# Router logits from un-normalised rows, and an expert's rows modulated as they are read from PSUM

## The chip, the cores and the metric

The kernel runs on one core of one Trainium2 chip. Five engines work side by side: TensorE (PE), VectorE (DVE), ScalarE (ACT), GpSimd (POOL), and SyncE (SP), which issues the weight DMAs. The metric is the device time of one execution in microseconds. Before the change it was 1742.97 us, the median of 3 runs (1740.7 to 1743.19).

## The reference

Two layers act on 256 latent tokens with a prefix of 256 context tokens, D = 1024. Each layer has a token mixer (differential attention beside a spatial gating part) and a channel mixer. In layer 1, the last, only the latent tokens go on, and the channel mixer is a mixture of experts. This is what the change touches:

```python
f_lat = modulate(rmsnorm(x_lat, pre_ffn_g[1]), ms[3], ms[4])     # h * (1 + scale) + shift
logits = t @ router_w                                            # 256 x 8
top_v, top_i = lax.top_k(logits, 2); top_w = softmax(top_v)
for e in range(8):
    y = y + gates[:, e:e+1] * ((silu(t @ w1[e]) * (t @ w3[e])) @ w2[e])     # D_EXPERT = 3584
x_lat = x_lat + ms[5] * rmsnorm(y, post_ffn_g[1])
```

Everything is float32.

## The kernel before

Each float32 product is done as three matmuls on halves of the operands: `hi` is the value rounded to the format fp32r, `lo` is the rest, and the product is hi*hi + lo*hi + hi*lo (`mm3`, L637 to L640). The weights arrive as units of 128x1024 float32 (512 KB, one DMA each). Of each unit ACT writes `w_hi` (L1239, for the experts L1560), DVE writes `w_lo` = unit - `w_hi` (L1657), and PE does 6 matmuls of 512 columns with them. `w_hi` and `w_lo` have SPL = 4 places, so ACT can split a unit only when PE has used the one four before it. For the experts 12 units are in flight from DRAM.

Each engine's order of work is written out by hand, and semaphores join the engines. The order in which the code of an engine calls the helpers below is thus the order in which its instructions run.

The router stage lies between the output projection of layer 1 and the experts. Two blocks of 128 token rows (tb = 0, 1) are normalised: ACT squares the output (L1499), DVE adds two partial sums and makes the mean (L2248, L2249), ACT takes the root (L1502), DVE inverts it and updates `xs` (L1926); then again square (L1257), mean (L1794), root (L1261), inverse and scaling to `xn` (L1799, L1801). PE transposes `xn` (`turn_h`, L710, with `keep_warm` matmuls L700, whose results nobody reads). ACT and DVE modulate the transposed rows, each four of eight 128x256 pieces, into `hT32` (L1314, L2280). PE computes the logits from these (L1076) and transposes the modulated rows back (L1086), and ACT copies them to `hrow` (L1618). `hrow` is what `gather_first` (L1103) and the scatter to DRAM (`xrows`, L619) read. DVE finds the two best experts of each token (L2127 to L2135: `mask_r`), PE counts ranks with small matmuls (L1091 to L1095), and DVE makes from them the 0/1 matrix `perm` of expert 0 (L2141), the rows' places in DRAM (`dest`, L2143 to L2151) and the gates (`token_gates`, L2157 to L2170).

Expert 0's rows come by a matmul with `perm`; those of the experts 1 to 7 are read from `xrows` into `xe` and transposed by PE into two PSUM banks (`gather`, L1130), just before the last four units of the expert ahead (`down(STEPS - 1)`). ACT then copies each bank to `he_hi` (L1541), and DVE subtracts to `he_lo` (L2177). One expert is 84 units: w1 and w3 pieces (`up`), and w2 pieces (`down`) behind them. PE starts an expert with `up(0, 0)`, which waits for unit 0's `w_lo` and for `he_lo`.

Of the kernel before, what the change touches and what calls it, by code (L numbers as in the profile page):

```python
# [17 lines left out]
F32 = mybir.dt.float32  # L18
# [7 lines left out]
P = 128  # L26
# [184 lines left out]
def program(nc, x, ctx, ada_w, ada_b, post_mix_g, post_ffn_g, w_in, w_out,  # L211
# [6 lines left out]
    with ExitStack() as stack:  # L218
# [23 lines left out]
        xs = place("xs", [P, NB, D], F32)  # L242
        cst = place("cst", [P, C_END], F32)
# [55 lines left out]
        rw = place("rw", [P, KD, 32], F32, Z + 36864)  # L299
        hrow = place("hrow", [P, NLAT, D], F32, Z)  # L300
# [4 lines left out]
        triu_r = place("triu_r", [P, P], F32R, H + 28928)  # L305
        ones_r = place("ones_r", [P, P], F32R, H + 29440)
        mask_r = place("mask_r", [P, 2 * NE], F32R, H + 29952)
        perm = place("perm", [P, NLAT, P], F32, H + 30208)
        perm_last = place("perm_last", [P, NLAT, P], F32, H + 31232)
        turned_last = by_expert = perm  # L310
# [130 lines left out]
        def _(sp):  # L441
# [35 lines left out]
            def experts(turn):  # L477
# [4 lines left out]
                def take_x(e):  # L482
                    sp.wait_ge(sg("gathered"), e * 2 + 2 * NE * turn)
                    sp.dma_start(xe[:, :], xv[e][turn]).then_inc(sg("xe in"), 16)
# [50 lines left out]
        def _(pool):  # L535
# [72 lines left out]
            spatial_params(1)  # L608
            spatial_norms(1)
            gate_rows(2)  # L610
            pool.wait_ge(unit_used, NS0)
            link(pool.memset(rw[:, :, :], 0.0))
            pool.dma_start(rw[:, :, 0:NE], router_w[0].rearrange("(k p) e -> p k e", p=P)).then_inc(sg("ws in"), 16)
            pool.wait_ge(sg("rows filled"), 32 * NE + 16)
            pool.wait_ge(sg("hrow"), NLAT)
            pool.wait_ge(sg("dest"), 1)
            for j in range(2):
                for tb in range(NLAT):
                    pool.indirect_dma_start(xrows[:, :], bass.IndirectOffsetOnAxis(ap=dest[:, NLAT * j + tb:NLAT * j + tb + 1], axis=0),  # L619
                                            hrow[:, tb, :], None).then_inc(sg("x sent"), 16)  # L620
# [15 lines left out]
        def _(pe):  # L636
# [64 lines left out]

            def turn_h(key, nb, ks=range(KD)):

                for b in range(nb):
                    if key == "ffn1":
                        keep_warm(12 if b else 6, ps[:, 7, P * b:P * b + P])
                    for k in ks:
                        if k % 4 == 0:
                            pe.wait_ge(sg("xn " + key), b + 1 + (b * k // 4 if key == "ffn1" else 0))
                        m = pe.transpose(ps[:, hT_bank(key, k), P * b:P * b + P], xn[:, b, P * k:P * k + P], ident)  # L710
                        if b == nb - 1:
                            m.then_inc(sg("hT ps " + key), 1)
# [251 lines left out]
            def project_out(l):  # L964
# [35 lines left out]
                pe.wait_ge(sg("z pm%d" % l), 2 * len(out_blocks(l)))  # L1000
# [68 lines left out]

            def route():  # L1070

                pe.wait_ge(sg("ws in"), 16 * 3)
                for k in range(KD):
                    pe.wait_ge(sg("hT32 odd ffn1" if k % 2 else "hT32 ffn1"), k // 2 + 1)
                    q = k % 4
                    m = pe.matmul(ps[32 * q:32 * q + 32, 0, 0:NLAT * P], rw[:, k, :], hT32_late[:, k, 0:NLAT * P], start=(k < 4), stop=(k >= 4),  # L1076
                                  tile_position=(0, 32 * q))
                m.then_inc(sg("logits"), 1)
                for tb in range(NLAT):
                    if tb:  # L1080
                        pe.wait_ge(sg("logits"), 2)
                        for half in range(NLAT):
                            m = pe.transpose(ps[:, half, 0:P], by_expert[:, half, :], ident)
                        m.then_inc(sg("logits"), 1)
                    for k in range(KD):
                        m = pe.transpose(ps[:, 4 + 2 * tb + k // 4, P * (k % 4):P * (k % 4) + P], hT32_late[:, k, P * tb:P * tb + P], ident)  # L1086
                    m.then_inc(sg("hT ps ffn1"), 1)
# [9 lines left out]
            def gather_first():  # L1097
# [3 lines left out]
                for k in range(KD):  # L1101
# [3 lines left out]
                    if k % 4 == 3:  # L1105
                        m.then_inc(sg("gathered"), 1)
# [1257 lines left out]
```

## Time and profile before

| | |
|---|---|
| median of 3 runs | 1742.97 us |
| the profiled execution | 1742.21 us |
| its span | 1740.4 us |
| mean granted clock of TensorE | 0.996 |
| busy: PE, DVE, ACT | 98%, 81%, 63% |
| router stage, end of the output projection to expert 0 at full pace | 757.2 to 783.7 us |
| experts | to about 1724 us |

The span is the part of the execution that the trace covers, here 1.8 us less than the execution's time. A busy PE is not PE at its peak: back to back, 512-column matmuls start every 0.23 us, while each row gives one of them 0.39 us.

### The profile page before, as it was taken

The page shows a single profiled execution, that of the slowest core. Times are in us where ns is not written, and L with a number is a line of the kernel's source. Part 1 is how long each engine was busy: PE and PEld are TensorE (multiplying, and loading weights), DVE is VectorE, ACT ScalarE, POOL GpSimd, SP SyncE. Part 2 cuts the span into 40 slices and gives each one's busy share as a digit, 9 for nine tenths or more (in the row PEclk, how much of TensorE's full clock was granted, in tenths as well). Part 3 has the DMA queues.
Part 4 walks back from the last instruction along what each step waited for, and adds up shares of the span by engine and source line. Part 5 has one row for each costly group of instructions (what it writes and reads, how often), then busy time and mean ns, then how long its engine had stood idle before and what let it go on. Part 6 is the DMA issues. An engine that isn't in the chain of part 4 may idle for free.

```text
span 1740.4 us, 24303 instructions
## 1 busy us (share of the span) xinstructions
PE 1702.7 (98%) x8034; PEld 1380.6 (79%) x8034; DVE 1406.1 (81%) x1655; ACT 1094.9 (63%) x1401; POOL 78.1 (4%) x92
## 2 busy tenths in 40 slices
PE   7999999999999999999999999999999999999997
PEld 4876878888788877778888888888888888888885
DVE  4947677385664589769999999999999999999998
ACT  4435552222222354658888888888888888888886
POOL 0114000000010000310000000000000000000001
PEclk9999999999999999999999999999999999999999
DMA  9858736364574447269999999999999999999995
GB/s 346 281 162 303 265 95 197 105 182 132 157 230 155 126 125 266 75 231 373 383 361 395 385 368 394 376 376 391 366 390 383 362 396 384 369 393 372 381 379 189
DMA packets 229200, 504.73 MB, mean 290 GB/s; under 512 B 16192, under 2 KB 47040, under 8 KB 228848
## 3 DMA queue, kind: packets, MB, share of 16 engines
q1 hardware_dynamic: 225152, 492.78, 79.2%
q0 software_dynamic: 3968, 10.94, 2.1%
q8 instruction: 44, 0.72, 0.2%
q14 instruction: 36, 0.29, 0.0%
HBM read 496.81 MB, written 19.95 MB: 297 GB/s over the span
## 4 chain that ended last, share of the span: by engine, by line
PE 93%; DVE 4%; ACT 1%; issue 1%; DMA 1%; SPq 1%; DVEq 0%; ACTq 0%
PE ps L638 29%; PE ps L640 28%; PE ps L639 28%; PE ps L1161 1%; PE ps L899 1%; PE ps L934 1%; DVE w_lo L1657 1%; DMA raw<-in_ada_w 1%; PE ps L922 0%; PE ps L665 0%; PE ps L658 0%; PE ps L1130 0%; PE ps L685 0%; PE ps L1103 0%; PE ps L882 0%
## 5 line engine op out<-in xcount | busy, mean ns | idle before, releaser
L1657 DVE TENSOR_TENSOR w_lo<-raw,w_hi 128x1024 fp32r<-128x1024 f32 x570 | 685.2, 1224 | 168.4 <-ACT w_hi L1239 141.1
L1560 ACT ACTIVATE w_hi<-raw 128x1024 fp32r<-128x1024 f32 x448 | 473.1, 1061 | 100.3 <-PE ps L640 100.2
L638 PE MATMUL ps<-w_hi,he_hi 128*128 128x512 f32 x896 | 353.7, 395 | 0.8 <-DVE w_lo L1657 0.8
L640 PE MATMUL ps<-w_hi,he_lo 128*128 128x512 f32 x896 | 349.5, 390 | 0.0
L639 PE MATMUL ps<-w_lo,he_hi 128*128 128x512 f32 x896 | 348.8, 389 | 0.0
L1657 DVE TENSOR_TENSOR w_lo<-raw_more,w_hi 128x1024 fp32r<-128x1024 f32 x224 | 273.6, 1225 | 31.1 <-ACT w_hi L1560 12.2
L1560 ACT ACTIVATE w_hi<-raw_more 128x1024 fp32r<-128x1024 f32 x224 | 237.8, 1062 | 50.8 <-PE ps L640 50.8
L1239 ACT ACTIVATE w_hi<-raw 128x1024 fp32r<-128x1024 f32 x122 | 128.4, 1059 | 195.7 <-PE ps L640 182.6
L640 PEld LDWEIGHTS ps<-w_hi,he_lo 128*128 128x128 f32 x896 | 168.2, 188 | 35.9
L638 PEld LDWEIGHTS ps<-w_hi,he_hi 128*128 128x128 f32 x896 | 168.2, 188 | 34.5 <-DVE w_lo L1657 1.2
L639 PEld LDWEIGHTS ps<-w_lo,he_hi 128*128 128x128 f32 x896 | 168.4, 188 | 33.8
L638 PE MATMUL ps<-w_hi,ae_hi 128*128 128x512 f32 x448 | 175.9, 393 | 0.0
L640 PE MATMUL ps<-w_hi,ae_lo 128*128 128x512 f32 x448 | 174.5, 390 | 0.0
L639 PE MATMUL ps<-w_lo,ae_hi 128*128 128x512 f32 x448 | 174.4, 389 | 0.0
L638 PE MATMUL ps<-w_hi,hT_hi 128*128 128x512 f32 x368 | 149.4, 406 | 2.7 <-DVE hT_lo L2057 1.5
L640 PE MATMUL ps<-w_hi,hT_lo 128*128 128x512 f32 x368 | 144.3, 392 | 0.0
L639 PE MATMUL ps<-w_lo,hT_hi 128*128 128x512 f32 x368 | 144.1, 392 | 0.0
L638 PE MATMUL ps<-hT_hi,w_hi 128*128 128x512 f32 x352 | 137.4, 390 | 1.0 <-DVE hT_lo L1825 1.0
L640 PE MATMUL ps<-hT_hi,w_lo 128*128 128x512 f32 x352 | 137.0, 389 | 0.0
L639 PE MATMUL ps<-hT_lo,w_hi 128*128 128x512 f32 x352 | 137.0, 389 | 0.0
L1674 DVE SCALAR_TENSOR_TENSOR acc<-raw,cstat,acc 128x1024 f32<-128x1024 f32 x84 | 105.2, 1280 | 1.7
L640 PEld LDWEIGHTS ps<-w_hi,ae_lo 128*128 128x128 f32 x448 | 84.1, 188 | 17.7
(276 smaller groups left out, 1962.9 us busy)
## 6 DMA issues: line engine op xcount, KB each, us to landing
raw<-in_moe_w SPq DMA_DIRECT2D x448, 512.0 KB, 6.0
raw_more<-in_moe_w SPq DMA_DIRECT2D x224, 512.0 KB, 5.9
raw<-in_ada_w SPq DMA_DIRECT2D x96, 512.0 KB, 4.4
raw<-in_ffn_w SPq DMA_DIRECT2D x66, 512.0 KB, 4.5
raw<-in_w_in SPq DMA_DIRECT2D x40, 512.0 KB, 5.6
raw<-in_w_out SPq DMA_DIRECT2D x16, 512.0 KB, 6.6
yrows<-in_x SPq DMA_DIRECT2D x9, 512.0 KB, 16.3
xe<-xrows SPq DMA_DIRECT2D x7, 512.0 KB, 6.5
```

The costliest lines, as they stand in the source:

```text
L638: pe.matmul(o, lh, rh, start=start, stop=False)
L639: pe.matmul(o, lh, rl, start=False, stop=False)
L640: return pe.matmul(o, ll, rh, start=False, stop=stop)
L899: m = pe.matmul(scores(l, t)[:, m_, :], qT[l][HD * m_:HD * m_ + HD, h, P * b:P * b + P], kT[HD * m_:HD * m_ + HD, h, k0:512], start=True, ...
L934: m = pe.matmul(ps[:, BANK_O, 0:P], wT[:, i % 2, P * kb:P * kb + P], proj[:, kb0 + kb, 2 * DA + P * h:2 * DA + P * h + P], start=(kb == 0) ...
L1161: m = pe.transpose(ps[:, 4 + s % 2, P * j:P * j + P], ae32[:, s % 2, P * j:P * j + P], ident)
L1239: act.activation(w_hi[:, u.s % SPL, :], raw_at(u.k), ACT.Copy).then_inc(hi_done, 1)
L1560: act.activation(w_hi[:, s % SPL, :], expert_raw(i), ACT.Copy).then_inc(hi_done, 1)
L1657: dve.tensor_tensor(w_lo[:, s_ % SPL, :], src, w_hi[:, s_ % SPL, :].bitcast(F32), ALU.subtract)\
L1674: ins = dve.scalar_tensor_tensor(out=total, in0=raw_at(u.k), scalar=cstat[:, k, r:r + 1], in1=total, op0=ALU.mult, op1=ALU.add)
```

## The change

1. **The router.** PE transposes the raw rows `xs` as soon as they are updated (`turn_x`), and not the normalised ones. The first four pieces of a block are copied from PSUM by DVE and the other four by ACT (`keep_xT`). The router's weights are multiplied beforehand by the modulation's scale (`rw_a`), and their product with its shift is summed (`rw_b`, `scale_router`, on DVE in the attention of layer 1). DVE gets the logits as (raw logit) * (1/rms of the row) + (shift's part).
2. **The rows.** What is gathered and scattered is `xn`, normalised but not modulated, so that the transposes back and `hrow` go. Each expert's rows are modulated as ACT reads them from PSUM: eight 128x128 pieces into `he32` in SBUF (Identity with a scale and a bias per partition), then a copy to `he_hi`; DVE subtracts from `he32`.
3. **The order in the router stage.** DVE splits unit 0 between the two blocks' top-2, units 1 to 3 between the pairs of `he_lo`, and makes `dest` and the gates after these. The `keep_warm` matmuls now stand before the ranks and before the gather.
4. **The means.** Wherever DVE made a mean from a sum of squares for ACT's root, ACT's root now takes scale 1/D and a bias (EPS, or the first half's sum prepared earlier by `rest`). This is in all norms but the spatial one and one pair in layer 0.
5. **Router weights** are loaded in layer 1's attention, once the rope tables that they overwrite have been used.

The core of the diff:

```diff
-            for i in range(2):
-                split_expert_unit(i, 0, 0)
-            modulate_h("ffn1", 1, 1, NLAT, range(0, KD, 2))
-            for i in range(2, AHEAD + 1):
-                split_expert_unit(i, 0, 0)
-            for tb in range(NLAT):
-                act.wait_ge(sg("hT ps ffn1"), KD + tb + 1)
-                act.activation(hrow[:, tb, :].rearrange("p (a n) -> p a n", a=2), ps[:, 4 + 2 * tb:6 + 2 * tb, :], ACT.Copy)\
-                    .then_inc(sg("hrow"), 1)
+            norm_before_experts()
+            for i in range(1, AHEAD + 1):
+                split_expert_unit(i, 0, 0)
...
+            def norm_before_experts():
...
+                    if tb:
+                        keep_xT(0)
+                        split_expert_unit(0, 0, 0)
...
+                        act.activation(xn[:, tb, o], xs[:, tb, o], ACT.Square, accum_out=st[:, 4 * half + tb:4 * half + tb + 1])\
+                            .then_inc(sg("ss ffn1"), 1)
+                    if tb:
+                        keep_xT(1)
...
+                act.wait_ge(sg("last rstd"), 1)
+                act.activation(xn[:, 1, :], xs[:, 1, :], ACT.Identity, scale=st[:, 13:14]).then_inc(sg("xn ffn1"), 1)
+
+            def split_first():
+
+                for pair in range(KD // 2):
+                    act.wait_ge(sg("gathered"), pair + 1)
+                    for k in (2 * pair, 2 * pair + 1):
+                        act.activation(he32[:, k, :], ps[:, 4 + pair, P * (k % 2):P * (k % 2) + P], ACT.Identity,
+                                       bias=mod_b[:, 1, 1, k, 0:1], scale=mod_a[:, 1, 1, k, 0:1]).then_inc(sg("he32"), 1)
+                    act.wait_ge(sg("he32"), 2 * pair + 2)
+                    act.activation(he_hi[:, 2 * pair:2 * pair + 2, :], he32[:, 2 * pair:2 * pair + 2, :], ACT.Copy).then_inc(sg("he hi"), 1)
+
+            def split_he(gathered, seen):
...
+                    act.wait_ge(sg("gathered"), gathered + (1 + half))
+                    for k in range(4 * half, 4 * half + 4):
+                        act.activation(he32[:, k, :], ps[:, 2 + half, P * (k % 4):P * (k % 4) + P], ACT.Identity,
+                                       bias=mod_b[:, 1, 1, k, 0:1], scale=mod_a[:, 1, 1, k, 0:1]).then_inc(sg("he32"), 1)
+                    act.wait_ge(sg("he32"), seen + (4 + 4 * half))
+                    act.activation(he_hi[:, 4 * half:4 * half + 4, :], he32[:, 4 * half:4 * half + 4, :], ACT.Copy).then_inc(sg("he hi"), 1)
...
             def pre_root(key, b):
-                act.wait_ge(sg("ms " + key), b + 1)
-                act.activation(st[:, 8 + b:9 + b], st[:, 4 + b:5 + b], ACT.Sqrt).then_inc(sg("rt " + key), 1)
+                act.wait_ge(sg("ss " + key), b + 1)
+                act.activation(st[:, 8 + b:9 + b], st[:, b:b + 1], ACT.Sqrt, scale=1.0 / D, bias=eps).then_inc(sg("rt " + key), 1)
...
+            def logits(tb, ks):
...
+                    m = pe.matmul(ps[:, (6, 3)[tb], 0:P], xT[:, tb, k, :], rw_a[:, k, :].unsqueeze(1).to_broadcast([P, P // NE, NE]),
+                                  start=(k == 0), stop=(k == KD - 1))
...
             def route():
...
+                turn_x(0, 0)
+                turn_x(0, 1)
+                logits(0, range(0, 6))
+                pe.wait_ge(sg("x mix1"), 3)
+                turn_x(1, 0)
+                pe.wait_ge(sg("x mix1"), 4)
+                turn_x(1, 1)
+                logits(0, range(6, KD))
+                logits(1, range(0, 4))
+                logits(1, range(4, KD))
...
+            def scale_router():
...
+                dve.tensor_tensor(rw_a[:, :, :], rw[:, :, :], mod_a[:, 1, 1, :, 0:1].to_broadcast([P, KD, NE]), ALU.mult)
...
+                link(dve.tensor_tensor(parts, rw[:, :, :], mod_b[:, 1, 1, :, 0:1].to_broadcast([P, KD, NE]), ALU.mult))
+                dve.tensor_reduce(rw_b[:, :], parts.rearrange("p k e -> p e k"), AX.X, ALU.add).then_inc(sg("rw scaled"), 1)
...
             def route():
...
+                    dve.wait_ge(sg("logits"), tb + 2)
+                    link(dve.scalar_tensor_tensor(out=lg[:, o], in0=ps[:, (6, 3)[tb], 0:NE], scalar=st[:, 12 + tb:13 + tb], in1=shifted[:, :],
+                                                  op0=ALU.mult, op1=ALU.add))
                     link(dve.max(mx[:, o], lg[:, o]))
                     link(dve.max_index(idx[:, tb, :], mx[:, o], lg[:, o]))
+                    if tb == 0:
...
+                        split_lo(NS0, expert_raw(0), NS0 + 1)
...
+            def split_first():
+
+                for i in range(1, AHEAD + 2):
+                    if i <= AHEAD:
+                        split_lo(NS0 + i, expert_raw(i), NS0 + i + 1)
+                    o = slice(2 * i - 2, 2 * i)
+                    dve.wait_ge(sg("he hi"), i)
+                    dve.tensor_tensor(he_lo[:, o, :], he32[:, o, :], he_hi[:, o, :].bitcast(F32), ALU.subtract).then_inc(sg("he"), 1)
...
+                    split_first()
+                    destinations()
                     token_gates()
```

At the end of an expert ACT ran the following, here for expert 0 (`ps` is PSUM, `ae_hi` the last activations of the expert, `raw` and `raw_more` the places of the units):

```order
L1560 ACTIVATE w_hi<-raw_more 128x1024
L1560 ACTIVATE w_hi<-raw 128x1024 x6
L1595 ACTIVATE ae_hi<-ps 128x512
L1560 ACTIVATE w_hi<-raw 128x1024 x2
L1541 ACTIVATE he_hi<-ps 128x512 x2
```

It now runs:

```order
L1614 ACTIVATE w_hi<-raw_more 128x1024
L1614 ACTIVATE w_hi<-raw 128x1024 x6
L1651 ACTIVATE ae_hi<-ps 128x512
L1614 ACTIVATE w_hi<-raw 128x1024 x2
L1593 ACTIVATE he_117<-ps,mod_b,mod_a 128x128 x4
L1596 ACTIVATE he_hi<-he_117 128x512
L1593 ACTIVATE he_117<-ps,mod_b,mod_a 128x128 x4
L1596 ACTIVATE he_hi<-he_117 128x512
```

The two copies of a bank have become eight modulated pieces and two copies from SBUF, still between the split of the last two units of one expert and of the first of the next.

PE in the router stage, from the end of the output projection to the gather of expert 0, before (`cst` holds the identity, `hT_77` is `hT32`):

```order
L700 MATMUL ps<-cst 128x128 x6
L710 MATMUL ps<-cst,xn 128x128 x8
L700 MATMUL ps<-cst 128x128 x12
L710 MATMUL ps<-cst,xn 128x128 x8
L1076 MATMUL ps<-hT_77,rw 32x256 x8
L1086 MATMUL ps<-cst,hT_77 128x128 x8
L1083 MATMUL ps<-cst,perm 128x128 x2
L1086 MATMUL ps<-cst,hT_77 128x128 x8
L1089 MATMUL ps<-triu_r,ones_r 128x128
```

and now:

```order
L1085 MATMUL ps<-rw_b,cst 128x8
L1067 MATMUL ps<-cst,xs 128x128 x8
L1077 MATMUL ps<-rw_a,xT 128x128 x6
L1067 MATMUL ps<-cst,xs 128x128 x8
L1077 MATMUL ps<-rw_a,xT 128x128 x10
L1098 MATMUL ps<-triu_r,ones_r 128x128
L704 MATMUL ps<-cst 128x128 x6
```

The transposes back and 18 of the matmuls that only keep PE busy (6 and 12) are gone from the front; 6 stand behind the logits, and 3 more behind the ranks.

DVE from the top-2 to the first units, before:

```order
L2141 TENSOR_SCALAR perm<-ps,rs 128x128 x2
L2143 TENSOR_TENSOR rs<-ps,rs 128x16
L2145 TENSOR_TENSOR rs<-rs 128x32
L2147 TENSOR_REDUCE rs<-rs 128x4
L2148 CAST dest<-rs 128x4
L2150 TENSOR_REDUCE rs<-ps 128x1
L2151 CAST flag<-rs 128x1
L1657 TENSOR_TENSOR w_lo<-raw_more,w_hi 128x1024
L2177 TENSOR_TENSOR he_lo<-ps,he_hi 128x512 x2
L1657 TENSOR_TENSOR w_lo<-raw_more,w_hi 128x1024
```

and now (the three `w_lo` are those of the units 1 to 3, each `he_lo` is a pair of 128-column pieces):

```order
L2213 TENSOR_SCALAR perm<-ps,rs 128x128 x2
L1708 TENSOR_TENSOR w_lo<-raw_more,w_hi 128x1024
L2253 TENSOR_TENSOR he_lo<-he_117,he_hi 128x256
L1708 TENSOR_TENSOR w_lo<-raw_more,w_hi 128x1024
L2253 TENSOR_TENSOR he_lo<-he_117,he_hi 128x256
L1708 TENSOR_TENSOR w_lo<-raw_more,w_hi 128x1024
L2253 TENSOR_TENSOR he_lo<-he_117,he_hi 128x256 x2
L2218 TENSOR_TENSOR rs<-ps,rs 128x16
L2219 TENSOR_TENSOR rs<-rs 128x32
```

The making of the rows' places (six rows, L2143 to L2151 before) stood ahead of the split of unit 2 and now begins, in the last two rows, behind unit 3 and the last pair of `he_lo`; the split of unit 0 stands further up, between the two blocks' top-2.

## Rows read from the trace of the kernel before

**Rows 1.** The page: each engine's busy time, share of the span, instructions.
```profile
PE 1702.7 (98%) x8034; PEld 1380.6 (79%) x8034; DVE 1406.1 (81%) x1655; ACT 1094.9 (63%) x1401; POOL 78.1 (4%) x92
```

**Rows 2.** Windows: from:to, length, busy of each engine, granted clock, DMA share, GB/s.
```profile
757.00:765.00 8.00, 6.20 (x53) 5.80 (x53) 5.75 (x13) 4.83 (x10) 1.42 (x2) 1.00 0.06 5
765.00:772.00 7.00, 5.02 (x40) 3.32 (x40) 5.64 (x23) 5.08 (x7) 0.00 (x0) 1.00 0.51 150
772.00:778.00 6.00, 5.93 (x35) 5.87 (x36) 2.69 (x8) 1.05 (x2) 3.52 (x4) 0.72 0.45 113
790.00:880.00 90.00, 90.00 (x410) 74.49 (x409) 84.05 (x77) 72.65 (x76) 0.00 (x0) 1.00 1.03 387
```

**Rows 3.** Chain of waits, 744 to 790: start, length, engine, tile, line.
```profile
756.94 0.24 PE ps L640
...
764.34 1.90 DVE hT L2280 x4
...
770.59 0.27 PE ps L1091
...
772.07 5.45 PE ps L1103 x32
...
782.45 1.24 DVE w_lo L1657
...
783.73 0.50 PE ps L638
```

**Rows 4.** Timeline of DVE in the router stage: start, length, instruction, idle and releaser.
```profile
758.19 0.68 DVE L2251 TENSOR_TENSOR zmix<-ps,gg 128x512 f32<-128x512 f32 x1
...
758.97 1.29 DVE L1926 SCALAR_TENSOR_TENSOR xs<-zmix,st,xs 128x1024 f32<-128x1024 f32 x1
...
771.84 0.17 DVE L2143 TENSOR_TENSOR rs<-ps,rs 128x16 f32<-128x16 f32 x1
...
772.95 1.22 DVE L1657 TENSOR_TENSOR w_lo<-raw_more,w_hi 128x1024 fp32r<-128x1024 f32 x1
...
779.92 0.15 DVE L2157 TENSOR_TENSOR rs<-ps,mask_r 128x2 f32<-128x2 f32 x1
```

**Rows 5.** Timeline of PE, same stage: the matmuls that only keep it busy.
```profile
761.24 2.84 PE L700 MATMUL ps<-cst 128*128 128x128 f32 x24
```

**Rows 6.** Timeline of ACT around the end of expert 0.
```profile
890.16 2.02 ACT L1560 ACTIVATE w_hi<-raw 128x1024 fp32r<-128x1024 f32 x2
892.09 1.07 ACT L1541 ACTIVATE he_hi<-ps 128x512 fp32r<-128x512 f32 x2
893.32 1.06 ACT L1560 ACTIVATE w_hi<-raw_more 128x1024 fp32r<-128x1024 f32 x1 [0.17 <-PE ps L640]
...
897.42 1.06 ACT L1560 ACTIVATE w_hi<-raw_more 128x1024 fp32r<-128x1024 f32 x1 [0.30 <-PE ps L640]
```

**Rows 7.** Timeline of DVE there.
```profile
893.52 1.28 DVE L2177 TENSOR_TENSOR he_lo<-ps,he_hi 128x512 fp32r<-128x512 f32 x2
894.72 5.02 DVE L1657 TENSOR_TENSOR w_lo<-raw_more,w_hi 128x1024 fp32r<-128x1024 f32 x4
```

**Rows 8.** Timeline of ACT in layer 1: modulated and plain 128x256 from PSUM.
```profile
643.92 3.76 ACT L1279 ACTIVATE hT<-ps,mod_b,mod_a 128x256 f32<-128x256 f32 x8 [3.00 <-PE ps L720]
...
738.82 1.21 ACT L1487 ACTIVATE hT_hi<-ps 128x256 fp32r<-128x256 f32 x4 [1.24 <-PE ps L961]
```

**Rows 9.** One line, L1528: minimum, median, maximum ns of a 128x512 SBUF copy.
```profile
L1528 ACT ACTIVATE at_hi<-a x22: 631/632/637, 274.8 to 586.2; 128x512 fp32r<-128x512 f32 x22
```

**Rows 10.** Waits of PE: us, times, longest, in 200 to 260.
```profile
PE ps L720 <- DVE zmix L2251: 1.8, 1, 1.8
```

**Rows 11.** Waits of PE in 600 to 660.
```profile
PE ps L720 <- DVE xn L1801: 1.3, 1, 1.3
```

**Rows 12.** Waits of PE in 660 to 757.
```profile
PE ps L961 <- DVE proj L2079: 0.3, 1, 0.3
```

**Rows 13.** Timeline of DVE in the last stage: the sum of two mean squares.
```profile
1731.85 0.15 DVE L2315 TENSOR_TENSOR st<-st 128x1 f32<-128x1 f32 x1
```

More of the change, by code:

```diff
@@ L1068, in ffn, with turn_x @@
                                 m.then_inc(unit_used, 1)
-            def route():
[L1072 to L1078, printed above, removed]
-                for tb in range(NLAT):
[L1080 to L1087, printed above, removed]
-                pe.wait_ge(sg("route consts"), 1)
+            def turn_x(tb, half):
+                bank = (4, 0)[tb] + half
+                for k in range(4 * half, 4 * half + 4):
+                    m = pe.transpose(ps[:, bank, P * (k % 4):P * (k % 4) + P], xs[:, tb, P * k:P * k + P], ident)
+                m.then_inc(sg("xT ps"), 1)
@@ new lines, in route @@
+            def route():
+                pe.wait_ge(sg("rw scaled"), 1)
+                pe.matmul(ps[:, 7, 0:NE], ones, rw_b[:, :], start=True, stop=True).then_inc(sg("logits"), 1)
+                pe.wait_ge(sg("x mix1"), 2)
+                turn_x(0, 0)
[8 more added lines that the diff above has]
+                logits(1, range(4, KD))
+                pe.wait_ge(sg("z pm1"), 2 * NLAT)
@@ L1491, in _ @@
                     post_square("pm%d" % l, 0, b, nb, ps[:, 2 * b, :], ptmp[:, 0:512])
-                for b in out_blocks(l):
+                for b in out_blocks(l) if l == 0 else ():
                     if b == nb - 1:
@@ new lines, in norm_before_experts @@
+            def norm_before_experts():
+                rest("pm1", NLAT)
+                for tb in range(NLAT):
+                    if tb:
+                        dve.wait_ge(sg("logits"), 1)
+                        dve.tensor_copy(shifted[:, :], ps[:, 7, 0:NE])
+                        dve.wait_ge(sg("xT ps"), 1)
+                        dve.tensor_copy(xT[:, 0, 0:4, :], ps[:, 4, :].rearrange("p (k t) -> p k t", t=P)).then_inc(sg("xT dve"), 1)
+                    dve.wait_ge(sg("ss pm1"), NLAT + tb + 1)
+                    dve.tensor_tensor(zmix[:, tb, 512:1024], ps[:, 2 * tb + 1, :], gg[:, gate_at(1, 0, 0), 512:1024], ALU.mult)\
+                        .then_inc(sg("z pm1"), 1)
+                    dve.wait_ge(sg("rt pm1"), tb + 1)
+                    link(dve.reciprocal(st[:, 28 + tb:29 + tb], st[:, 24 + tb:25 + tb]))
+                    dve.wait_ge(sg("z pm1"), NLAT + tb + 1)
+                    for half in range(2):
+                        o = slice(512 * half, 512 * half + 512)
+                        dve.scalar_tensor_tensor(out=xs[:, tb, o], in0=zmix[:, tb, o], scalar=st[:, 28 + tb:29 + tb], in1=xs[:, tb, o],
+                                                 op0=ALU.mult, op1=ALU.add).then_inc(sg("x mix1"), 1)
+                    dve.wait_ge(sg("ss ffn1"), 2 * tb + 1)
+                    dve.tensor_scalar(st[:, 57 + tb:58 + tb], st[:, tb:tb + 1], 1.0 / D, EPS, ALU.mult, ALU.add).then_inc(sg("rest ffn1"), 1)
+                    if tb:
+                        dve.wait_ge(sg("xT ps"), 3)
+                        dve.tensor_copy(xT[:, 1, 0:4, :], ps[:, 0, :].rearrange("p (k t) -> p k t", t=P)).then_inc(sg("xT dve"), 1)
+                    else:
+                        dve.wait_ge(sg("rt ffn1"), 1)
+                        link(dve.reciprocal(st[:, 12:13], st[:, 8:9]))
+                        dve.wait_ge(sg("x mix1"), 2)
+                        dve.tensor_scalar(xn[:, 0, :], xs[:, 0, :], st[:, 12:13], None, ALU.mult).then_inc(sg("xn ffn1"), 1)
```

228 lines of the change are left out of this document (112 added, 116 removed).

## The prediction, made before the changed kernel was run

> **What bounds the kernel now.** I read the page first, then the windows by stage, then the chain of waits and the timelines around the two places that the change touches. TensorE is busy for 98% of the span, DVE for 81%, ACT for 63% [rows 1], and in 90 us of the experts PE is busy all 90 at a granted clock of 1.00 [rows 2]. So work taken from DVE or ACT gives nothing unless it ends a wait of PE, and work added to them costs nothing until PE waits. There are two kinds of place where PE can gain or lose.
>
> The first is the router stage. The output projection ends at 757.2 and PE is at full pace at 783.7, where the matmuls of unit 0 begin [rows 3]: 26.5 us of little else than the chain from norm to transposes, modulation (DVE's four pieces at 764.34, 1.90 us), logits, ranks (770.59), gather (772.07, 5.45 us), and finally `w_lo` of a unit at 782.45. The matmuls that only keep PE busy stand in this gap, for example 2.84 us of them at 761.24 [rows 5]; so PE's 5.02 busy of 7.00 in 765 to 772 is no sign that it is the limit there [rows 2].
>
> The second is the end of each expert. PE never waits there now, but ACT is close: behind the two `he_hi` copies it was idle only 0.17 us before PE released the place of the next unit, against 0.30 at the units after it [rows 6]. ACT has about 0.3 us to spare in each unit of 1.36 us (start to start, 896.06 to 897.42), and at this spot 0.17.
>
> **The router stage, part by part.** The chain up to the second block's `xs` stays: DVE's product of 0.68 at 758.19 and the update of 1.29 at 758.97 [rows 4], the update now in two halves, so PE can start transposing after the first. I rebuilt the stage with the durations of before. Block 1's `xs` is done at about 760.5; eight transposes and the copies of four pieces by DVE and four by ACT (one 128x512 copy from PSUM is half of the 1.07 us pair [rows 6], about 0.55) and the last matmuls put the logits of block 0 at about 761.7 and of block 1 at about 763.5. Between them DVE does the top-2 and `w_lo` of unit 0 (1.22 [rows 4]). Then top-2 of block 1 and the one-hots: the ranks at about 765.1, where they were at 770.59 [rows 3], 5.5 us earlier. What went is the norm's second half, the modulation (1.90) and the trip through the logits' layout. Scaling `xn` moves beside the top-2 and is hidden by it.
>
> The gather then starts at about 766.6. It took 5.45 us for 16 products (32 records) while the granted clock was 0.72 in 772 to 778, a mean between the full 2.4 and the half 1.2 GHz, and 1.00 in the 15 us before [rows 2, 3]. At the warm rate of 0.24 us each (2.84 us for 12 [rows 5]; its pitch is nearer 0.22) it would take 3.6. ACT follows by pairs of pieces: two modulated (0.35 each, worked out below), a wait and a copy, 1.2 us a pair against PE's 0.9, so `he_hi` is done at about 772.5. DVE no longer does the rows' places (1.1 us, 771.84 to 772.95 [rows 4]) and the gates (2.5 us, 779.92 to 782.45 [rows 3, 4]) in front of these splits as a whole: the places have moved behind unit 3, the gates still stand ahead of the `w_lo` for which PE waits at 783.7, the fifth unit. That one now ends near 772.9 + 1.1 + 2.5 + 1.24 = 777.7. **6.0 us won**. Bounds: 7.5, if the copies and waits overlap better than I let them, and 4, if the gather is as slow as now and one link of the chain is later by half a microsecond. If the clock should fall already in the ranks the 5.45 us of gather at 0.72 would grow, and the first units with it: the gather alone is 3.7 us more if it runs at half the warm rate (16 at 0.45 instead of 0.22). The matmuls that keep PE busy are 9 behind the logits now, where 18 stood before them; I take the clock as holding for the logits and give its fall a rival.
>
> `scale_router` (three small operations and three copies, about 1 us of DVE in the attention of layer 1) and the weights' DMA on POOL I cost at nothing: PE's waits from 660 to 757 that DVE ends at the projection are 0.3 us in all [rows 12]. If that cover is gone it is at most that 1 us. The scatter to DRAM starts later on DVE's side (places behind unit 3) and earlier by the stage; expert 1's rows are needed at the end of expert 0, which no router wait reaches.
>
> **The means.** Each takes two operations of 0.15 to 0.19 us off DVE (the sum of 0.15 at 1731.85 [rows 13]) where ACT's root waited for them. What counts is where PE waits at the end of such a chain: 1.8 us once at layer 0's mixer norm [rows 10], 0.35 of it goes; 1.3 us once before layer 1 [rows 11], behind two blocks with three such operations each, of which I take 1.15; 0.3 for the projection [rows 12], which I take whole; and two operations in the last stage, 0.4. **2.2 us won**, with 1 and 3.5 as bounds: 1 if what comes next late (POOL's part, the weights' splits) takes most of it, 3.5 if all waits of these rows go.
>
> **The ends of the experts.** Nothing in the trace shows a modulated 128x128 piece. Eight modulated 128x256 took 3.76 us, so with a last one of about 0.57 they start 0.455 apart; four plain ones 1.21, so 0.27 apart [rows 8]. The pointers cost about 0.19. Half of 256 columns is 0.10 less: 0.35 apart, the last 0.46 long. A bank is 3 x 0.35 + 0.46, a hop of 0.04, and the copy of 128x512. From SBUF such a copy took 0.63 long [rows 9], from PSUM 0.58 with the next 0.49 behind; I take 0.53. That is 2.08 a bank and 4.16 for two, where the two copies took 1.07 (0.98 to what follows). **ACT has 3.2 us more between the last units of an expert and the first of the next**, and PE waits for the latter.
>
> The sum for expert 0's end: 892.09 [rows 6] + 4.16 = 896.25; `w_hi` 1.06, so 897.31; `w_lo` behind it 1.23 (four in 5.02 [rows 7]), so 898.55. PE is ready for the new unit at about 897.2: its last matmul on the old expert's last unit is what let ACT's fourth `w_hi` start at 897.42 [rows 6], a hop behind it. It waits 1.35 us, with `he_lo` done well before. ACT and DVE, at 0.96 us (two in 2.02 [rows 6]) and at most 1.26 a unit, then gain on PE's 1.36 and nothing follows. There are seven such ends, and PE has no idle time in an expert to win it back from: 7 x 1.4 = **10 us lost**. Bounds: with pieces at the plain price (0.27 less 0.10, so 0.17 each) ACT is 1.4 us sooner and PE does not wait: 0. At the full 256-column price (0.455 each, 0.1 x 8 more) it waits 2.2: 15 us. I take the middle, as it is the measured modulated operation with only its columns reduced.
>
> ACT's price for such a piece is what the Trainium skill also gives ("ScalarE: Activation LUTs", What ACT_TABLE_LOAD costs): a fixed 186 ns, 0.833 ns a column, 93 ns more for each per-partition pointer, with 93 ns hidden back to back. By that page a modulated 128x128 is 479 ns long and the next starts 386 ns behind it; for 128x256 it says 585, and this case's trace has about 0.57. By the page's price each end would cost 1.7 us, an estimate, and the seven 12 us. The sum goes by the rows.
>
> **The sum.** -6.0 - 2.2 + 10.0 = +1.8 on the profiled execution's 1742.21: 1744.0. The median of the runs lies 0.8 above that execution, so between 1744.0 and 1744.8: I say 1744.4. About 0.2%, 3.5 us, is what can be told from no change here, so the likeliest case is no change: 1739.5 to 1746.5.
>
> **The rivals.**
>
> A. The case above: front gains and boundary stalls cancel. Chance 0.45.
>
> B. The ends cost little: pieces overlap more than in the rows, or PE is ready later than 897.2. It decides below about 0.8 us an end. With 0.5 us each, 3.5 us in all: 1742.2 - 8.2 + 3.5 = 1737.5. For it: I have no row of a 128x128 piece; against it: ACT's slack there is 0.17 us, and it gets 3.2 more. 0.17.
>
> C. The ends cost more: the price of 0.455 a piece, 2.2 us each, 15 in all: 1742.2 - 8.2 + 15.4 = 1749.4. This is the other side: slower, and it decides from 1.65 us an end. For it: the hop from the last piece to the copy, twice, and ACT's later copy of the expert's output, which also stands ahead of a unit. Against it: half the columns must cost less. 0.20.
>
> D. The clock falls in the router stage. Fewer matmuls, and short ones, stand there, and it fell to 0.72 even before, 11 us after 761 with 24 records of them. Then the gather takes up to 3.7 us more and the stage gives 2.3 instead of 6: 1742.2 - 2.3 - 2.2 + 10 = 1747.7. 0.13. Of the clock the Trainium skill says ("TensorE: Matmul & The Clock Gate", Part 4: PE-mode transpose) that a transpose does not count as busy for the clock in the way a matmul does. By that page the 16 new ones in front of the logits would not help to hold it, which would speak for this rival; no row of before tells transposes from the matmuls beside them.
>
> E. The logits are not earlier, since both copies of a block wait behind other work on DVE and ACT: 2 us less won, 1746.5. 0.05.
>
> The predicted time is A's. The range, 1738.5 to 1750.0, reaches B's and C's centres. Faster by over 0.2% (under 1739.5) is most of B: 0.15. Slower (above 1746.5) is C, D and a tail of A: 0.37. Within: 0.48.
>
> **What the profile after would show.** Seven waits of PE for `w_lo` at the first unit of the experts 1 to 7, 1.2 to 1.6 us each; over 1.9 means C, under 0.8 means B. Modulated 128x128 pieces 0.35 apart. The ranks about 8 us behind the output projection's end (13.4 now) and full pace about 20.5 behind it (26.5 now). The granted clock in the gather tells D. PE's waits at the mixer norm of layer 0 and before layer 1 are shorter by 0.35 and about 1.1. I am wrong in the main if PE does not wait at the ends of the experts, or if the router stage is not at least 4 us shorter.

## The result, and the profile after

The changed kernel takes 1749.85 us (median of 6, 1749.38 to 1750.77), the one before beside it 1742.24: a ratio of 1.0048, 95% interval 1.0039 to 1.0058. It is 7.6 us slower. I had forecast no change at 1744.4, with 0.37 for slower.

The page after, the line that answers to [rows 1], and in section 4 the chain's shares by engine:

```profile
PE 1701.5 (97%) x8016; PEld 1378.8 (79%) x8016; DVE 1402.5 (80%) x1627; ACT 1117.7 (64%) x1468; POOL 78.0 (4%) x91
...
PE 90%; DVE 4%; ACT 3%; issue 2%; DMA 1%; SPq 0%; ACTq 0%; DVEq 0%
```

ACT has 23 us more than before, and its share of the chain went from 1% to 3%. The waits of PE from 790 to 1750 (line, releaser, us in all, times, longest) say where; before, there was in the same stretch one wait, for `ysb`, of 0.7:

```profile
PE ps L642 <- DVE w_lo L1708: 9.2, 7, 1.8
PE ps L1134 <- issue: 2.3, 1, 2.3
PE ps L1134 <- ACT ysb L1607: 0.7, 1, 0.7
```

Two things are new: seven waits at the ends of the experts, which the prediction has, and one of 2.3 us in the last stage, which it has not. For the whole account I took the n-th matmul of the helper `mm3` in each trace (512 columns each; there are 6720 in both) and compared the starts:

| place | before | after | after minus before |
|---|---|---|---|
| first of layer 0's channel mixer | 252.02 | 251.28 | -0.74 |
| nine matmuls later | 254.17 | 254.99 | +0.82 |
| beside the norm that opens layer 1 | 621.16 | 620.84 | -0.32 |
| last stretch of the output projection | 739.19 | 738.48 | -0.71 |
| expert 0 at full pace | 783.73 | 777.29 | -6.44 |
| start of expert 1 | 897.22 | 892.68 | -4.54 |
| start of expert 2 | 1015.78 | 1012.75 | -3.03 |
| start of expert 7 | 1608.54 | 1612.96 | +4.42 |
| two matmuls later, and to the last one | 1608.99 | 1613.54 | +4.55 |
| the end of the span | 1740.4 | 1748.6 | +8.2 |

So: -0.7 up to the router, -5.7 in the router stage, +11.0 at the ends of the experts, +3.6 behind the last expert.

**The router stage.** The windows after (from:to, length, busy of PE, PEld, DVE, ACT, POOL with counts, granted clock, DMA share, GB/s), against [rows 2]:

```profile
757.00:765.00 8.00, 7.42 (x62) 6.70 (x60) 6.71 (x21) 7.12 (x15) 0.00 (x0) 1.00 0.09 9
765.00:769.00 4.00, 4.00 (x35) 3.84 (x35) 2.37 (x6) 2.77 (x7) 0.00 (x0) 1.00 0.46 141
769.00:775.00 6.00, 6.00 (x32) 5.05 (x31) 5.59 (x19) 5.84 (x13) 0.97 (x1) 1.00 0.70 214
```

The clock is at its full level throughout, where it was 0.72 in the gather. PE's timeline there (start, length, engine, line, tiles, idle before):

```profile
764.59 0.27 PE L1101 MATMUL ps<-mask_r,ones_r 128*128 128x8 f32 x1 [0.23 <-DVE mask_r L2207]
...
766.07 3.81 PE L1114 MATMUL ps<-perm,xn 128*128 128x128 f32 x32
...
777.29 0.50 PE L642 MATMUL ps<-w_hi,he_hi 128*128 128x512 f32 x1 [1.95 <-DVE w_lo L1708]
```

The ranks start 8.3 us behind the projection's end (756.3), the gather takes 3.81 instead of the 5.45 of [rows 3], and the wait for the fifth unit's `w_lo` ends at 777.29.

**The end of an expert**, here of expert 1, on ACT, then what PE waits for; against [rows 6, 7]:

```profile
1004.30 2.00 ACT L1614 ACTIVATE w_hi<-raw 128x1024 fp32r<-128x1024 f32 x2
1006.19 1.50 ACT L1593 ACTIVATE he<-ps,mod_b,mod_a 128x128 f32<-128x128 f32 x4
1007.72 0.63 ACT L1596 ACTIVATE he_hi<-he 128x512 fp32r<-128x512 f32 x1
1008.26 1.49 ACT L1593 ACTIVATE he<-ps,mod_b,mod_a 128x128 f32<-128x128 f32 x4
1009.78 0.63 ACT L1596 ACTIVATE he_hi<-he 128x512 fp32r<-128x512 f32 x1
1010.31 3.88 ACT L1614 ACTIVATE w_hi<-raw_more 128x1024 fp32r<-128x1024 f32 x4
```
```profile
1011.11 0.39 PE L644 MATMUL ps<-w_hi,ae_lo 128*128 128x512 f32 x1
1012.75 0.49 PE L642 MATMUL ps<-w_hi,he_hi 128*128 128x512 f32 x1 [1.25 <-DVE w_lo L1708]
```

The modulated pieces start 0.342 us apart and one is 0.455 long (medians of 56). A bank takes 2.06, both 4.12: 1006.19 to 1010.31. Then come `w_hi` and `w_lo` of the next unit, and PE starts 1.51 us later than it did.

**Behind the last expert.** The rows of PE that place the last rows of `ysb`, before and after, and a window after:

```profile
1727.34 3.70 PE L1123 MATMUL ps<-ysb,perm 128*128 128x512 f32 x8 [0.69 <-ACT ysb L1553]
```
```profile
1731.88 0.70 PE L1134 MATMUL ps<-ysb,perm 128*128 128x512 f32 x1 [0.69 <-ACT ysb L1607]
1734.83 4.97 PE L1134 MATMUL ps<-ysb,perm 128*128 128x512 f32 x7 [2.25 <-issue]
```
```profile
1735.50:1738.50 3.00, 3.00 (x6) 1.26 (x5) 1.52 (x3) 1.45 (x4) 0.00 (x0) 0.59 0.00 0
```

Eight records that took 3.70 together now take 0.70, a wait of 2.25 that ends with nothing that the profile shows ("issue"), and 4.97, in whose middle 3 us the mean granted clock is 0.59: from start to end 7.92 instead of 3.70, +4.2. What comes behind them is 0.6 shorter. What moved in that stretch is seen in the DMA queues of 1732 to 1733 (packets, MB, share):

```profile
q8 instruction: 1, 0.02, 7.8%
q14 instruction: 1, 0.01, 2.5%
```

Both are packets of instructions. In the trace before, such a pair starts in 1727 to 1728, and PE does not stop. The packets alone are thus no sign of a stop: in all thirteen traces of this case a packet of q8 starts within 0.8 us of the first of the eight records, and PE stops in two of them.

### The profile page after: what moved, and what is told of

The parts are those of the page before. It is cut to its first block, busy times and chain, and to the rows that moved or that the text cites. A ratio compares the mean times of both kernels' runs of the same rounds, so it can differ in the third digit from the quotient of the medians.

```text
span 1748.6 us, 24328 instructions
## 1 busy us (share of the span) xinstructions
PE 1701.5 (97%) x8016; PEld 1378.8 (79%) x8016; DVE 1402.5 (80%) x1627; ACT 1117.7 (64%) x1468; POOL 78.0 (4%) x91
## 4 chain that ended last, share of the span: by engine, by line
PE 90%; DVE 4%; ACT 3%; issue 2%; DMA 1%; SPq 0%; ACTq 0%; DVEq 0%
PE ps L642 28%; PE ps L644 27%; PE ps L643 27%; PE ps L1173 1%; PE ps L891 1%; DVE w_lo L1708 1%; ACT he L1593 1%; PE ps L926 1%; ACT w_hi L1614 1%; DMA raw<-in_ada_w 1%; PE ps L914 0%; PE ps L669 0%; PE ps L689 0%; PE ps L1134 0%; PE ps L751 0%
```

## The experiments

Each ran on the chip with runs of the kernel before beside it; the ratio is to these. To compare the experts and not the last stage, most carry the edit of the first, which I call the old code position.

**1. Code position, taken back.** In PE's branch for an overfull expert, which is not executed (69 waits, by my count 35 instructions, two waits in each):

```diff
                 experts(1)
+                for _ in range(69):
+                    pe.wait_ge(sg("flag set"), 1)
                 pe.wait_ge(sg("y copied"), 2 * NE)
```

> The changed kernel with 35 more instructions of PE (semaphore waits) in the branch for an overfull expert, which is not taken: nothing more is executed, but the code behind the branch, the last stage's, stands as far into PE's program as in the kernel before (which has 18 matmuls more, two instructions each, and one wait less). Theory 1, the 2.25 us wait of PE in the last rows is the fetching of its code, which now falls between two of the last eight matmuls: the wait goes, the clock stays at 1.00 there, the eight take 3.7 us again, and the kernel takes 3.6 to 4 us less than the changed one, ratio to before about 1.002. Theory 2, the wait comes from the changed data flow (ACT's copies or the later rows): 1.0048 and the wait stays at 2.2 us.

1746.37 us, ratio 1.0028 (1.0017 to 1.0038); the changed kernel's was 1.0048 (1.0039 to 1.0058), so 3.5 us less. PE's row there:

```profile
1732.69 3.70 PE L1134 MATMUL ps<-ysb,perm 128*128 128x512 f32 x8 [0.69 <-ACT ysb L1609]
```

The wait is gone and the eight take 3.70, in one piece, with nothing executed being different.

**2. Code position, brought into the kernel before.** The same edit with 441 waits (221 instructions by the same count) in the kernel before.

> The kernel before with 220 instructions more in PE's branch that is not taken: its last stage then stands 36 instructions short of where 256 more would put it, as the changed kernel's stands 35 short of the one before. Theory 1 (code position, with a pattern that repeats within 256 instructions): a wait of about 2.2 us of PE between two of the last eight matmuls, a lower clock behind it, 3.5 to 4 us slower than before, 1.002. Theory 2: the time of before, no such wait.

1745.64 against 1741.26, ratio 1.0025 (1.0016 to 1.0034), with

```profile
1726.76 0.70 PE L1123 MATMUL ps<-ysb,perm 128*128 128x512 f32 x1 [0.78 <-ACT ysb L1555]
1730.13 5.92 PE L1123 MATMUL ps<-ysb,perm 128*128 128x512 f32 x7 [2.67 <-issue]
```

The same stop after the same first matmul, 2.67 long, and a slow rest, at a granted clock of 0.54 in 1730 to 1736. Both directions agree: the position of PE's code costs 3.5 to 4.4 us here by the medians (4.2 and 5.4 in the traces, from the first of the eight to the end), with nothing that is executed being different. That PE waits for the fetch of its own instructions is the likely reading; no trace shows it, since a packet of q8 passes there whether PE stops or not. Where exactly the pattern lies within PE's program I did not map: the positions 35 instructions short of the kernel before's and 221 beyond it stop, that of the kernel before doesn't.

**3. The means alone**, in the kernel before (all hunks of part 4, none of the others); one of them:

```diff
-                act.wait_ge(sg("ms " + key), b + 1)
-                act.activation(st[:, 8 + b:9 + b], st[:, 4 + b:5 + b], ACT.Sqrt).then_inc(sg("rt " + key), 1)
+                act.wait_ge(sg("ss " + key), b + 1)
+                act.activation(st[:, 8 + b:9 + b], st[:, b:b + 1], ACT.Sqrt, scale=1.0 / D, bias=eps).then_inc(sg("rt " + key), 1)
```

> The kernel before with the change's fourth part alone: ACT's root makes the means, everywhere but in the spatial norm and the pair of layer 0. Theory as predicted: 2.2 us less (waits before layer 0's mixer norm 1.8 to 1.5, before layer 1 1.3 to 0.4, 0.4 in the last stage), 1740.0 and ratio 0.9987. Rival, what the changed kernel's trace shows: up to 1.5 us of it are lost again to a lower granted clock at the start of layer 0's channel mixer (0.77 in 248 to 254 us), ratio 0.9996; if the low clock comes from the earlier norm it is in this trace too.

1740.62, ratio 0.9996 (0.9987 to 1.0005): from 2.3 us won to 0.9 lost. The forecast of 2.2 is just inside; it is neither confirmed nor refuted. Its waits are shorter as forecast, against the 1.3 of [rows 11]:

```profile
PE ps L720 <- DVE xn L1810: 0.4, 1, 0.4
```

Its trace had the full clock in layer 0. So had the first experiment's, which has the same norms, while in the changed kernel's the clock was 0.77 from 248 to 254, and in that of the next experiment 0.87. It was full in all six later traces that have this norm unchanged. The fall is thus not a fixed consequence of the means; it came in two executions of ten and cost 1.56 us in the changed kernel's trace (the table's -0.74 to +0.82).

The router stage of this trace is 1.9 us shorter than before, though only the making of the means was changed in it. Most of that is the gather, which had the full clock here and took 3.81 us as in the changed kernel:

```profile
769.38 3.81 PE L1103 MATMUL ps<-perm,hrow 128*128 128x128 f32 x32 [0.76 <-DVE perm L2126]
```

In the two traces with the norm of before (the kernel before and experiment 2) it took 5.44. So the change of the router isn't needed for the full clock in the gather. Whether the shorter wait of PE ahead of this norm (1.50 us for 1.76) holds it, or the single execution decides, these traces don't tell. The traced execution, 1737.76, was 2.9 us below its median.

**4. The ends without modulation** (the experts 1 to 7 get unmodulated rows, and DVE subtracts from PSUM again), at the old code position:

```diff
-                    for k in range(4 * half, 4 * half + 4):
-                        act.activation(he32[:, k, :], ps[...], ACT.Identity, bias=..., scale=...).then_inc(sg("he32"), 1)
-                    act.wait_ge(sg("he32"), seen + (4 + 4 * half))
-                    act.activation(he_hi[...], he32[...], ACT.Copy).then_inc(sg("he hi"), 1)
+                    act.activation(he_hi[...], ps[:, 2 + half, :].rearrange(...), ACT.Copy).then_inc(sg("he hi"), 1)
```

> The changed kernel with the code position of the first run, and with the rows of the experts 1 to 7 copied plainly from PSUM at the ends of the experts, as before: their modulation is left out. Theory, the eight modulated pieces cost all of what is lost in the experts: PE has no wait at the seven ends, 11.0 us less than the first run, ratio about 0.9957. Rival, part of it is something else that the change did to the experts (the rows' later scatter, DVE reading from SBUF): waits of some tenths are left, and less than 9 us are won.

1734.62, ratio 0.9957 (0.9942 to 0.9973), 11.7 us less than the first experiment, and PE has no wait from 790 on but the 0.7 for `ysb`. An expert takes 118.55 us from start to start, as in the kernel before, against 120.06 in the first experiment. The eight pieces are the whole loss in the experts, as forecast. It also bounds the rest of the change: 6.6 us under the kernel before (4.7 to 10.1 by the interval of four runs) for router and means together, 0.6 of it the means by the third experiment. That agrees with the router stage's 5.7 in the traces, within wide bounds.

**5. Pieces without scale and bias** (plain copies of 128x128, again without the modulation):

> The same pieces of 128x128 by ACT, but plain copies without scale and bias: the modulation of the experts 1 to 7 is left out. By the rows of the kernel before (plain 128x256 pieces 0.27 us apart, less 0.10 for half the columns) they start 0.17 us apart; by the Trainium skill's page ScalarE: Activation LUTs, 186 ns + 107 ns, 93 ns hidden, it is 0.20. Eight of them are then 1.2 to 1.4 us shorter than the modulated ones 0.345 apart, and PE's waits at the ends fall from 1.25 to 0 to 0.15 us. Rival: it is the number of instructions that counts, not the pointers: 0.30 apart or more, waits of 0.9 us or more.

One run, 1737.95, 8.4 us less than the first experiment's median. ACT's row at the end of expert 1:

```profile
1006.53 0.77 ACT L1595 ACTIVATE he<-ps 128x128 f32<-128x128 f32 x4
1007.33 0.64 ACT L1597 ACTIVATE he_hi<-he 128x512 fp32r<-128x512 f32 x1
```

One piece is 0.278 long, and they start 0.157 apart (medians of 56). So the modulation costs 0.342 - 0.157 = 0.185 us a piece, 1.5 in eight, and an expert takes 118.62 us instead of 120.06. PE's wait fell to 0.3 us, once. The function changed with the pointers, from Identity to Copy; the two are not told apart here. The Trainium skill's 93 ns for each pointer ("ScalarE: Activation LUTs", What ACT_TABLE_LOAD costs) agrees with these 0.185 us for two; its lengths are 15 to 24 ns too long for these shapes (293 for 278, 479 for 455), and the measurement decides: by the page an end would have cost 1.7 us, an estimate, and it cost 1.5.

**6. DVE modulates the second bank.**

```diff
+                dve.wait_ge(sg("gathered"), n + 2)
+                for k in range(4, 8):
+                    dve.tensor_scalar(he32[:, k, :], ps[:, 3, P * (k % 4):P * (k % 4) + P], mod_a[:, 1, 1, k, 0:1],
+                                      mod_b[:, 1, 1, k, 0:1], ALU.mult, ALU.add).then_inc(sg("he32 dve"), 1)
```

> The changed kernel at the code position of the one before, and at the end of an expert DVE modulates the four pieces of the second bank (PSUM to SBUF, a scale and a bias per partition) while ACT modulates those of the first; ACT makes both copies to he_hi. Theory, ACT's 4.12 us between the last unit of an expert and the first of the next are what PE waits for: ACT's time falls to 4 x 0.35 + 0.11 + 0.04 + 0.53 + 0.54 = about 2.6, 1.5 us less, just what PE lost at each end (1.50 from the second on), so the waits go to 0 to 0.3 us, 9 to 11 us are won on the first run (pad35), and the kernel is faster than before, ratio 0.996 to 0.998. Rival, DVE is the next to be late (it is busy 93% of the time in an expert and gets about 1.2 us more at each end): PE waits 0.5 us or more for w_lo all the same, ratio 0.999 or above.

ACT keeps the four pieces of the first bank and both copies. 1742.87, ratio 1.0009 (1.0000 to 1.0018), 3.5 us less than the first experiment. It is the rival: PE still waits 0.5 us or more for `w_lo` at each end, and the ratio is above 0.999. ACT waits now:

```profile
1005.04 1.50 ACT L1596 ACTIVATE he<-ps,mod_b,mod_a 128x128 f32<-128x128 f32 x4
1006.57 0.63 ACT L1599 ACTIVATE he_hi<-he 128x512 fp32r<-128x512 f32 x1
1007.89 0.63 ACT L1599 ACTIVATE he_hi<-he 128x512 fp32r<-128x512 f32 x1 [0.70 <-DVE he L2262]
1008.43 3.89 ACT L1617 ACTIVATE w_hi<-raw_more 128x1024 fp32r<-128x1024 f32 x4
```

DVE was still splitting the last two units and began its pieces at 1006.50. ACT's time from the pieces to the next unit is 3.39 instead of 4.12, and PE's waits are 4.2 us in seven instead of 9.2.

**7. The same with 15 instead of 12 matmuls** that only keep PE busy in layer 0's norm.

> The kernel ends_dve with 15 instead of 12 matmuls in the norm of layer 0's channel mixer, in the 0.9 us that PE waits there for the rows of the last block (248.3 to 249.2 us in the changed kernel). In two of four traces with the shorter norm the granted clock fell there (0.77 and 0.87 in 248 to 254 us) and cost 1.5 us, in two it didn't. Theory, the gaps of PE there let the clock fall and the matmuls close one: clock 1.00 there, and on the mean 0.5 to 1 us less than ends_dve. Rival: no difference that can be told.

1742.47, 1.0007 (0.9998 to 1.0016): no difference that can be told. The clock in 248 to 254 was full in this trace and in the sixth experiment's, so the two traces don't test the matmuls.

**8. No such matmuls in the router stage:**

```diff
-                keep_warm(6, ps[:, 7, 0:P])
...
-                keep_warm(3, ps[:, 7, 0:P])
```

> The changed kernel at the code position of the one before, without the 9 matmuls of the router stage whose results nobody reads (6 behind the logits, 3 behind the ranks). Theory: they keep the clock at full speed for the gather (1.00 in 765 to 769 us); without them the granted clock falls in the gather or the first units, the gather takes up to 3.8 us more and the kernel 1 to 4 us more than the first run. Rival: the transposes, logits and ranks are enough, clock 1.00 and the same time as the first run.

1746.28, 1.0029 (1.0019 to 1.0038), the first experiment's time and not 1 to 4 us more. In the trace the clock falls, but most of the cost is missing:

```profile
757.00:763.00 6.00, 4.55 (x39) 4.13 (x37) 5.21 (x18) 5.20 (x10) 0.00 (x0) 1.00 0.02 4
763.00:770.00 7.00, 6.05 (x38) 6.00 (x39) 4.43 (x10) 4.82 (x10) 0.00 (x0) 0.76 0.51 147
```
```profile
PE ps L1100 <- DVE mask_r L2207: 1.6, 1, 1.6
PE ps L642 <- DVE w_lo L1708: 1.4, 1, 1.4
```

The clock falls from full to a mean of 0.76 after PE has waited 1.6 us for the mask, and the gather takes 5.44. That is 1.6 us more than 3.81, but PE then waits 0.5 us less for the fifth unit (1.4 against 1.9), and from the projection's last matmul to full pace the stage is 22.36 us (754.66 to 777.02) against 21.22 in the first experiment's trace (756.90 to 778.12): 1.1 us more. The medians do not show it, and their intervals are too wide to exclude it. Such a fall, which is rival D's, costs here a third of the 3.7 that D gave it, since part of the gather is hidden behind ACT and DVE.

**9. Everything four units earlier.** PE transposes the next rows ahead of `down(STEPS - 2)`, and DVE's pieces stand ahead of the last `ae_lo`:

```diff
+                        if s == STEPS - 1 and not last:
+                            gather(e * 16 + 16 * (NE * turn + 1))
                         if s:
                             down(s - 1)
-                    if not last:
-                        gather(e * 16 + 16 * (NE * turn + 1))
```

> As ends_dve, and the next expert's rows are transposed four units earlier (ahead of down(STEPS - 2)), and DVE modulates its four pieces ahead of the last ae_lo, so that they are there when ACT has copied the first bank. In ends_dve ACT waited 0.70 us for DVE's fourth piece, and PE 0.5 to 0.6 us for w_lo at each end. Theory, those 0.7 us of ACT are the rest of what PE waits for: PE's waits at the ends go to 0 to 0.1 us, 4 to 5 us less than ends_dve, ratio to before 0.998 (0.997 to 0.9985). Rival, DVE's pieces now make ae_lo late: a wait of PE for ae_lo or w_lo of up to 0.6 us an end takes the place, ratio 1.000 or above.

1746.49, 1.0028 (1.0018 to 1.0038): the rival, and dearer than it said. PE's waits from 780 on, beside the one for `ysb`:

```profile
PE ps L642 <- DVE ae_lo L2294: 8.1, 7, 1.2
```

**10. DVE's pieces behind `ae_lo`**, else the same.

> As ends_early, with DVE's four pieces behind the last ae_lo instead of ahead of it, and ahead of the splits of the expert's last two units. Theory: ae_lo is in time again (done at 1003.97 us in ends_dve, where PE needed it at 1004.6), the pieces end at about 1005.3, ahead of ACT's first copy (to 1007.2), and the last two units' w_lo come 1.3 us later than in ends_dve, at 6.4 and 7.6, where PE takes them at 7.4 and 8.7: no wait of PE over 0.1 us at an end, 4 to 5 us less than ends_dve, ratio to before 0.998 (0.997 to 0.9985). Rival: one of DVE's splits is late after all, waits of 0.3 us or more an end, ratio 1.000.

1741.89, 1.0004 (0.9995 to 1.0013), 1.0 less than the sixth and about the rival's time. PE's waits at the ends are 1.8 us in seven, but an expert takes 119.44 us from start to start (118.55 before). In the sixth it took 119.34, so the 1.0 us does not come from the experts. The transposes in their old place had covered the making of `ae_hi` and `ae_lo`, and ACT, with four pieces and two copies, is still 0.2 late.

**11. The transposes in halves:** DVE's four early, ACT's four in the old place.

> As ends_mid, with the transposes of an expert's rows in two parts: the four pieces that DVE modulates as early as in ends_mid (ahead of down(STEPS - 2)), the four of ACT where they always were (ahead of down(STEPS - 1)). In ends_mid an expert took 119.43 us from start to start (1009.51 to 1128.94) against 118.56 before, though PE waited only 0.24 us at its end; 0.27 of the rest lies ahead of down(STEPS - 1), where the eight transposes had covered the making of ae_hi and ae_lo. Theory: four transposes (0.4 us) cover it again, an expert takes 119.0 us or less, 3 us less than ends_mid, ratio to before 0.9985 to 0.999. Rival: ACT, which starts its pieces no sooner, is the limit, 119.3 to 119.4 again and ratio 1.0005.

1739.78 us against 1741.29, ratio 0.9991 (0.9982 to 1.0000), 2.1 less than the tenth. An expert takes 119.01 (1009.01 to 1128.02), as forecast. PE's waits from 780 on, beside the one for `ysb`:

```profile
PE ps L642 <- DVE w_lo L1720: 0.3, 1, 0.3
```

This is 10 us better than the changed kernel, 3.5 of it by the code position, and level with or a little ahead of the one before. It isn't the 6 us ahead that the router stage gives. Each expert still takes 0.46 more than before, 3.2 in seven; the rest is within the intervals.

## Why the prediction was wrong

- **The last stage is the step that failed.** I had 0.4 us won there, from two operations fewer. It lost 3.6. PE has 18 matmul records fewer (8034 to 8016) and one wait more, by which, as I count, all its later code moved by 35 instructions; PE then stopped 2.25 us between two matmuls of the last stage and went on at a lower clock. Experiment 1 takes the stop away and 2 makes one, with nothing executed being different. That it is a fetch of instructions is likely and not shown. I looked at what PE's removed instructions cost to execute (nothing) and not at what stands behind them in the program. Without it the changed kernel is at 1.0028, about 5 us slower.
- **The ends of the experts** were right in mechanism and mis-sized by a tenth: ACT's 4.16 us measured 4.12, the piece of 0.35 measured 0.342, PE's 1.4 an end measured 1.51 (2.0 at the first, where ACT also stood 0.37 us with "issue"). The 0.1 I missed in each is PE's restart: its first matmuls after a wait start 0.33 apart instead of 0.23 (1012.75 and 1013.08). Sum 11.0 for 10.0. My lower bound for the ends, no stall at the plain price, was nearly met when the pieces were plain (experiment 5).
- **The router stage** was right: 5.7 won for 6.0, ranks at 8.3 us for 8, `he_hi` done at 771.9 for 772.5, full pace at 777.3 for 777.7. The last two are flattered by a stage that began 0.7 earlier than the one before. The clock held, as I took it, and 1.6 of the 5.7 are the gather in 3.81 instead of 5.44; by experiment 3 that part can come without the new router. That its fall would cost 3.7 (rival D) was too much: experiment 8 has the fall, and it costs 1.1. On transposes the Trainium skill's rule ("TensorE: Matmul & The Clock Gate", Part 4: PE-mode transpose) has no test in these runs: with them but without the nine matmuls the clock fell (experiment 8), which it allows, but a wait of 1.6 us lay there too.
- **The means** were forecast at 2.2. The waits of PE shrank as said (1.8 to 1.5, 1.3 to 0.4, 0.3 to none), and between equal matmuls the changed kernel's trace won 0.74, 1.14 and 0.39 up to the router. But alone they gave 0.6 us in the medians, with 2.3 and -0.9 as bounds. In the changed kernel's own trace the low clock behind layer 0's norm took 1.56 of them. How much they are worth on the mean stays open.
- **The chances.** The measured time lies in my range, and beyond my 1746.5. Rivals C and D, on which most of my chance for slower rested, were not the reason: C's 2.2 us an end was 1.5. Without the last stage's stop it is about 5 us slower, also beyond the 3.5: there the forecast of no change (+1.8) failed by errors of one sign, 1.0 at the ends, 0.3 in the router stage and about 1.6 at the means, to which the code's position added 3.5. The range itself was set wrong at its lower end: it was to reach B's centre, 1737.5, and stopped at 1738.5.

## What to carry to other kernels

Price an edit on a gap-free stretch by its slack: ACT had 0.17 us to spare where eight short operations went in, and seven such places outweighed 6 us won once. A helper's operation should be moved to where both its engine and the operation that waits have room, and whatever stands in its old place may be hiding something (here eight transposes hid the split of `ae`). And when instructions are removed or added, look at the engine's later code too: a wait of PE that ends with "issue" between two like matmuls can be a matter of position, and a few instructions in a branch that isn't taken show whether it is. The same part of two single traces can differ by 1.5 us through the clock alone, so such a difference should be looked for in further traces before it is put down to the edit.

## What the runs showed of the hardware

- Between the first and the second of eight matmuls PE stood 2.25 us (2.67 in experiment 2), depending on the position of its code alone: 69 waits in a branch that isn't taken remove it. It went with a mean clock of 0.59 behind it (0.54 in experiment 2). Packets of instructions pass at this place in all thirteen traces, with the stop and without.
- The granted clock behind a short gap of PE varies from execution to execution of nearly the same program: 0.77, 0.87 and eight times 1.00 in 248 to 254 us of ten kernels with the same norm. In the gather it was full in experiment 3 and low in the two traces with the norm of before, at 3.81 and 5.44 us. A difference of 1.5 us in one trace need not be the change's.
- Two per-partition pointers, with Identity in place of Copy, cost ACT 0.185 us of 0.342 for a 128x128 piece from PSUM. On DVE the same operation is 0.40 long and four take 1.35.
